# Two transformer blocks on one core: who sums the squares of a norm, who writes its diagonal, and where the rms of the first feed-forward goes

## What is computed

```python
def rmsnorm(x, g):
    y = x * lax.rsqrt(jnp.mean(x * x, axis=-1, keepdims=True) + EPS)
    return y * g

def first_block(x, ...):                       # 512 tokens
    for layer in range(2):
        h = rmsnorm(x, pre_norm[layer])
        if layer == 0:
            y = (retention(rope(q), rope(k), v) * silu(gate)) @ w_out_a   # q, k, v, gate from h @ w_in_a
        else:
            kv = rmsnorm(x, kv_norm) @ w_kv    # k (with rope) and v
            y = (rmsnorm(diff_attention(q, k, v, lam), sub_norm) * silu(gate)) @ w_out_b
        x = x + rmsnorm(y, post_norm[layer])
    return x

def swiglu(x, w_gate, w_up, w_down):
    return (silu(x @ w_gate) * (x @ w_up)) @ w_down

def second_block(x, ...):
    h = concatenate([meta, x])                 # 528 tokens
    h = h + 0.5 * swiglu(rmsnorm(h, ffn1_norm), ...)
    u = rmsnorm(h, mix_norm)                   # then mla(u) and gated_deltanet(u), merged by gates
    h = h + merged @ w_out
    h = h + 0.5 * swiglu(rmsnorm(h, ffn2_norm), ...)
    return rmsnorm(h, final_norm)[:, 16:]
```

## Time and profile before

| | before |
|---|---|
| median of three runs, us | 2071.51 (2068.78 to 2074.17) |
| profiled execution, us | 2070.14 |
| its span in the profile, us | 2068.1 |
| TensorE busy, us | 2013.0 (97%) |
| weight loads busy, us | 1760.6 (85%) |
| VectorE busy, us | 1093.9 (53%) |
| ScalarE busy, us | 838.6 (41%) |
| GpSimd busy, us | 599.9 (29%) |
| mean granted TensorE clock | 0.996 |

### The profile page before, as it was taken

One profiled execution on the slowest core, in us unless ns is written; L12 is line 12 of the kernel. 1 busy time (PEld: TensorE's weight loads), 2 busy tenths in 40 slices (PEclk: granted clock), 3 DMA queues, 4 the chain that ended last, 5 costly groups with the idle time before them and its releaser, 6 DMA issues. The chain is left out here.

```text
span 2068.1 us, 33871 instructions
## 1 busy us (share of the span) xinstructions
PE 2013.0 (97%) x14432; PEld 1760.6 (85%) x14432; DVE 1093.9 (53%) x1618; ACT 838.6 (41%) x1330; POOL 599.9 (29%) x207
## 2 busy tenths in 40 slices
PE   8999999999999999999999999999999999999998
PEld 6899888778977688999999878898777787999897
DVE  4400576236256737774656242266566556847473
ACT  6332222336456634452435344343222333444353
POOL 4443332444320134211202322034235243020202
PEclk9999999999999999999999999999999999999999
DMA  5323121222311121323232431132113121423331
GB/s 177 100 84 111 58 77 61 93 80 82 102 62 42 42 62 42 110 89 108 83 123 82 104 90 44 32 99 62 43 58 119 62 82 61 138 87 113 100 99 57
DMA packets 170062, 171.64 MB, mean 83 GB/s; under 512 B 16940, under 2 KB 160680, under 8 KB 169912
## 3 DMA queue, kind: packets, MB, share of 16 engines
q1 hardware_dynamic: 168508, 167.25, 25.8%
q10 hardware_dynamic: 1404, 2.23, 0.3%
HBM read 163.17 MB, written 6.29 MB: 82 GB/s over the span
## 5 line engine op out<-in xcount | busy, mean ns | idle before, releaser
L784 POOL TENSOR_TENSOR w_lo<-w_raw,w_hi 128x2048 fp32r<-128x2048 f32 (+2 forms) x117 | 493.7, 4223 | 1018.7 <-ACT w_hi L927 592.2
L2367 PE MATMUL ps<-u_hi,w_hi 128*128 128x512 f32 (+2 forms) x1480 | 477.1, 343 | 11.5 <-DVE sg L1867 3.3
L2367 PE MATMUL ps<-u_hi,w_lo 128*128 128x512 f32 (+2 forms) x1472 | 470.3, 339 | 0.0
L2367 PE MATMUL ps<-u_lo,w_hi 128*128 128x512 f32 (+2 forms) x1472 | 462.9, 339 | 1.0 <-DVE u_lo L1520 0.8
L2367 PEld LDWEIGHTS ps<-u_hi,w_hi 128*128 128x128 f32 x1480 | 267.7, 189 | 41.8 <-issue 5.5
L2367 PEld LDWEIGHTS ps<-u_lo,w_hi 128*128 128x128 f32 x1472 | 265.1, 189 | 31.2 <-DVE u_lo L1520 5.5
L2367 PEld LDWEIGHTS ps<-u_hi,w_lo 128*128 128x128 f32 x1472 | 266.6, 189 | 27.7 <-issue 0.5
L927 ACT ACTIVATE w_hi<-w_raw 128x2048 fp32r<-128x2048 f32 (+2 forms) x157 | 247.8, 1580 | 64.1 <-PE ps L2367 58.1
L2367 PE MATMUL ps<-hidden_hi,w_hi 128*128 128x264 f32 (+1 forms) x528 | 140.9, 321 | 1.3 <-DVE hidden_lo L1850 1.3
L2367 PE MATMUL ps<-hidden_lo,w_hi 128*128 128x264 f32 (+1 forms) x528 | 140.9, 321 | 0.0
L2367 PE MATMUL ps<-hidden_hi,w_lo 128*128 128x264 f32 (+1 forms) x528 | 140.6, 320 | 0.0
(11 more groups left out here) (423 smaller groups left out, 4010.6 us busy)
## 6 DMA issues: line engine op xcount, KB each, us to landing
w_raw<-in_w_in_a SPq DMA_DIRECT2D x22, 1024.0 KB, 5.2
w_raw<-in_ffn_w_gate SPq DMA_DIRECT2D x22, 1024.0 KB, 5.3
w_raw<-in_ffn_w_up SPq DMA_DIRECT2D x22, 1024.0 KB, 5.3
w_raw<-in_ffn_w_down SPq DMA_DIRECT2D x24, 768.0 KB, 4.5
w_raw<-in_w_in SPq DMA_DIRECT2D x17, 1024.0 KB, 5.3
w_raw<-in_w_out_a SPq DMA_DIRECT2D x8, 1024.0 KB, 5.1
w_raw<-in_w_kv SPq DMA_DIRECT2D x8, 1024.0 KB, 5.4
w_raw<-in_w_in_b SPq DMA_DIRECT2D x8, 1024.0 KB, 5.4
```

The lines of the kernel that those rows point to most:

```text
L784: pool.tensor_tensor(WL[:, u % RAWS, part], RAW[:, u % RAWS, part], WH[:, u % SPLITS, part].bitcast(F32), ALU.subtract).then_inc(lo_done, 1)
L2367: return nc.tensor.matmul(o, a, b, start=start, stop=stop, **kw)
```

## The change

- In post0 and post1, VectorE adds only the first seven squares. TensorE sums that (`two_sums`), runs 2 fillers in place of 5, and sums the eighth square straight from `SQ`, into the same columns.
- In ffn1, VectorE adds no squares. TensorE sums each of the eight squares as it comes (`square_sums`), inside the first unit, between the hi and the lo products of each contraction step. The final sums and the 9 fillers go. `spread_after` becomes 4: no slot is set aside, and the spread goes to columns 264 to 439 of three banks (three pieces of 176), behind step k = 3 of the second unit's chunk m = 0. The copy of the rms reads it there, and the bank of that slot is released with the first of the normalising instructions.
- The diagonal of post0, norm1, post1, ffn1, mix and ffn2 goes from ScalarE to VectorE (`diagonal_on_vector`), as products of the broadcast identity with the broadcast root, in two pieces (three in ffn1); the spread waits for each piece on its own. norm0, cq and ckv stay with ScalarE.
- ScalarE's order in ffn1: each square follows its `u_hi`, and the conversion of the first coming weight follows the eight squares.

```diff
-            ffns[name] = [(job(part, spread_after=3 if name == "ffn1" and n == 0 else None), job(4, kc=part))
+            ffns[name] = [(job(part, spread_after=4 if name == "ffn1" and n == 0 else None), job(4, kc=part))
...
+        not_added = {norms[name][3] + KC - 1 for name in ("post0", "post1", "ffn1")}
+        def added_upto(q):
+            return len([x for x in range(q + 1) if x not in not_added])
+        PIECES = {"ffn1": 3}
+        def pieces_of(name):
+            return 1 if name in ("norm0", "cq", "ckv") else PIECES.get(name, 2)
+        def diags_before(name):
+            return sum(pieces_of(x) for x in list(norms)[:norms[name][0]] if x != "final")
...
+            if name == "ffn1":
+                return PS[:, 2:5, 264:440]
...
-            diagonal("post0")
             for k in range(KC):
                 act.wait_ge(res_done, k + 1)
                 u_hi("norm1", k)
             for k in range(KC):
                 squares_after("norm1", k)
-            diagonal("norm1")
...
-                    next_hi(jg, 0, j)
+                    if (name, j) != ("ffn1", 0):
+                        next_hi(jg, 0, j)
...
-            diagonal("post1")
             for k in range(KC):
                 act.wait_ge(res_done, KC + k + 1)
                 u_hi("ffn1", k)
-            for k in range(KC):
                 squares_after("ffn1", k)
-            diagonal("ffn1")
+            hi(ffns["ffn1"][0][0].unit0 + 2)
             ffn_act("ffn1", 0, "mix")
-            diagonal("mix")
...
+            def diagonal_on_vector(name):
+
+                n, cols = norms[name][:2]
+                k, w = token_tiles(width_of(cols))
+                g = k // pieces_of(name)
+                dve.wait_ge(root_done, n + 1)
+                dve.wait_ge(nb_done, n)
+                for a in range(pieces_of(name)):
+                    nc.vector.tensor_tensor(DIAG[0:w, a * g * w:(a + 1) * g * w].rearrange("p (t c) -> p t c", t=g),
+                                            IDENT[0:w, 0:w].unsqueeze(1).to_broadcast([w, g, w]),
+                                            STAT[0:w, 2, a * g:(a + 1) * g].unsqueeze(2).to_broadcast([w, g, w]),
+                                            ALU.mult).then_inc(diag_done, 1)
...
+                    nc.vector.tensor_copy(RSTDB[:, 0:width].rearrange("p (a n) -> p a n", a=3),
+                                          spread_over(name)).then_inc(rb_done, 1)
...
                 rstd(name)
+                diagonal_on_vector(name)
...
+                    if after != "ffn1":
+                        add_square(q0 + k, k == 0, width_of(cols))
                 rstd(after)
+                diagonal_on_vector(after)
...
-            for k in range(KC):
+            for k in range(KC - 1):
...
+                    if k == 0 and name == "ffn1":
+                        slot, _ = spread_chunk(ffns[name][0][0])
+                        last.then_inc(ps_free[slot], 1)
...
             rstd("mix")
+            diagonal_on_vector("mix")
...
             rstd("ffn2")
+            diagonal_on_vector("ffn2")
...
+                                if after == "ffn1" and not high:
+                                    square_sums(after, k)
...
-                            if jb.spread_after is not None and k == kc - 2:
-                                slot_free(pe, *spread_chunk(jb))
-                                norm_sums(after)
-                            if jb.spread_after is not None and k == kc - 1:
-                                keep_clock(2 * spread_chunk(jb)[0], 9)
                             if k == kc - 1 and after == "norm1":
                                 norm_sums(after)
-                            elif k == kc - 1:
+                            elif k == (SPREAD_K if after == "ffn1" else kc - 1):
                                 norm_spread(after)
...
+            def square_sums(name, k):
+
+                _, cols, _, before, _ = norms[name]
+                count, w = token_tiles(width_of(cols))
+                pe.wait_ge(sq_done, before + k + 1)
+                for t in range(count):
+                    last = mm(sums_at[0:w, t:t + 1], SQ[:, (before + k) % 2, t * w:(t + 1) * w], ONES[:, 0:1],
+                              start=(k, t) == (0, 0), stop=k == KC - 1, skip_group_check=True)
+                last.then_inc(ns_done if k == KC - 1 else sq_added, 1)
+
+            def two_sums(name, between):
+
+                n, cols, squares, before, _ = norms[name]
+                k, w = token_tiles(width_of(cols))
+                pe.wait_ge(sq_added, added_upto(before + KC - 2))
+                for t in range(k):
+                    mm(sums_at[0:w, t:t + 1], SUMSQ[:, t * w:(t + 1) * w], ONES[:, 0:1], start=t == 0, stop=False,
+                       skip_group_check=True)
+                between()
+                pe.wait_ge(sq_done, before + KC)
+                for t in range(k):
+                    last = mm(sums_at[0:w, t:t + 1], SQ[:, (before + KC - 1) % 2, t * w:(t + 1) * w], ONES[:, 0:1],
+                              start=False, stop=True, skip_group_check=True)
+                last.then_inc(ns_done, 1)
...
-                pe.wait_ge(diag_done, n + 1)
-                o = spread_over(name)
-                if k == NT:
-                    last = mm(o, ONES[0:w, :], DIAG[0:w, 0:SEQ])
-                else:
-                    for a in range(2):
-                        last = mm(o[:, a, :], ONES[0:w, :], DIAG[0:w, HALF * a:HALF * (a + 1)])
+                o, made = spread_over(name), pieces_of(name)
+                parts = 2 if k > NT and made == 1 else made
+                size = k * w // parts
+                for a in range(parts):
+                    pe.wait_ge(diag_done, diags_before(name) + min(a + 1, made))
+                    last = mm(o[:, a, :] if k > NT else o[:, a * size:(a + 1) * size], ONES[0:w, :],
+                              DIAG[0:w, a * size:(a + 1) * size])
                 last.then_inc(nb_done, 1)
...
-            keep_clock(idle_bank, 5)
-            norm_sums("post0")
+            two_sums("post0", lambda: keep_clock(idle_bank, 2))
             keep_clock(idle_bank, 10)
```

More of the change, by code:

```diff
@@ L77, in build @@
         FIRST, LAST = 16512, 229344
+        SPREAD_K = 3
         ends, starts = {None: FIRST}, {}
@@ L407, in build @@
                    "mix": 6 * KC, "ffn2": 7 * KC, "final": 8 * KC, "cq": QN_ROW, "ckv": KVN_ROW}
+        not_added = {norms[name][3] + KC - 1 for name in ("post0", "post1", "ffn1")}
[6 more added lines that the diff above has]
+            return sum(pieces_of(x) for x in list(norms)[:norms[name][0]] if x != "final")
         def gain(name, k):
             return GAINS[:, gain_of[name] + k:gain_of[name] + k + 1]
-        slot, _ = spread_chunk(ffns["ffn1"][0][0])
+        first_slots = [(ffns["ffn1"][0][0].chunk0 + n) % SLOTS for n in range(4)]
         cq_bank = 2 * (j_cq.chunk0 % SLOTS) + 1
-        assert slot == 0 and cq_bank == 5
+        assert first_slots == [1, 2, 3, 0] and spread_chunk(ffns["ffn1"][0][0])[0] == 1 and cq_bank == 5
         spread_banks = {"post0": [2 * ((j_kv_k.chunk0 + 2) % SLOTS) + 1],
                         "post1": [2 * ((ffns["ffn1"][0][0].chunk0 + 2) % SLOTS) + 1],
-                        "ffn1": [2 * slot, 2 * slot + 1], "mix": [cq_bank, cq_bank + 2], "cq": [cq_bank - 2],
+                        "mix": [cq_bank, cq_bank + 2], "cq": [cq_bank - 2],
                         "ckv": [cq_bank - 4, cq_bank - 2]}
         def spread_over(name):
+            if name == "ffn1":
+                return PS[:, 2:5, 264:440]
             banks = spread_banks.get(name, [1])
@@ L969, in square @@
                 if q >= 2:
-                    act.wait_ge(sq_added, q - 1)
+                    act.wait_ge(sq_added, added_upto(q - 2))
                 nc.scalar.activation(halves(SQ[:, q % 2, 0:width]), src, ACT.Square).then_inc(sq_done, 1)
@@ L1465, in _ @@
                     squares_after("ffn2", 2 * j + m)
-            diagonal("ffn2")
             ffn_act("ffn2", 1, "final")
@@ L1482, in add_square @@
                 else:
-                    dve.wait_ge(sq_added, q)
+                    dve.wait_ge(sq_added, added_upto(q - 1))
                     nc.vector.tensor_tensor(SUMSQ[:, 0:width], SUMSQ[:, 0:width], SQ[:, par, 0:width],
@@ L2519, in norm_sums @@
                 else:
-                    pe.wait_ge(sq_added, before + squares)
+                    pe.wait_ge(sq_added, added_upto(before + squares - 1))
                 for t in range(k):
@@ L2681, in _ @@
             idle_bank = next(b for b in (3, 5, 7) if b not in spread_banks["post1"])
-            keep_clock(idle_bank, 5)
-            norm_sums("post1")
+            two_sums("post1", lambda: keep_clock(idle_bank, 2))
             keep_clock(idle_bank, 10)
```

5 lines of the change are left out of this document (removed).

## The result

The changed kernel took 2075.32 us (median of 19 executions, 2070.68 to 2078.18) against 2071.51: a ratio of 1.0015, interval 1.0008 to 1.0022, so slower by a little, and clear of noise. The profiled execution took 2072.63 us, its span is 2070.7. (One correction to what stands ahead of the prediction: a call of `keep_clock` is two passes in the trace, not four, and the four matmuls of a sum are eight; the prediction counted them right.)

A forecast was written before the change was run, and what follows sets the result against it. TensorE was taken as the bound, busy nearly the whole span. Posts -1.4, norm1 +1.2, ffn1 -0.4, mix 0 and ffn2 +0.75 give +0.15 us on the 2071.51 median: 2071.7 predicted, range 2067.0 to 2076.0.

The forecast's parts named there:

- the collision: At norm1, ffn1, mix, ffn2: GpSimd's 4.60 us split starts behind the root and holds VectorE's diagonal until it ends.
- Rival (a): The port does not hold the diagonals, as VectorE's requests get in first: -3.5 us, 2068.0; chance 0.17.
- The posts: post0 and post1: earlier sums, fewer fillers and VectorE's diagonal start the spread 0.7 us earlier each, bounds 0.2 and 1.1.
- norm1: Held diagonal, then second split on the diff_rope scaling: third kv_k unit +1.85 us, 0.6 given back later, +1.2 in all.
- ffn1: Final sums and fillers go, square sums enter the first unit, held diagonal idles TensorE: -0.4 us, or -3.5 if nothing held.
- the price of the twelve passes: ffn1's first unit: square sums add 0.89 us to each contraction step of 1.47, making 2.36; bounds 0.89 and 1.03.
- The wait at the spread: ffn1: the first diagonal piece comes only at the split's end, 808.15, so TensorE idles 3.1 us.
- ffn2 and mix: ffn2's held diagonal makes TensorE 0.75 us later; mix's comes in time even if held a whole split: 0.
- the half clock behind before's wait: ffn1: 0.50 of full clock in 811 to 814 counted as removed; 1.45 us to add if it halves again.
- rival (b): norm1's second split slips between the diagonal pieces, 2.4 us worse (2074.1); with half clock in ffn1 2075.5; chance 0.16.
- (c): Single-column passes in ffn1's first unit let the clock fall there, some 10 us more: 2082; chance 0.05.
- (d): Squares cheaper or spare columns free more; posts at 1.1, nothing held, norm1 0, ffn1 -4: -6.5, 2065.0; chance 0.04.

The follow-up runs named there:

- GpSimd behind VectorE: Changed kernel with GpSimd's splits waiting for VectorE's diagonal (norm1, ffn1, ffn2) and for the rotation table's scalings: 2063.10 us (0.9968), again 2062.31 us (0.9961).
- norm1's diagonal alone: Kernel before, with only norm1's diagonal moved from ScalarE to VectorE: 2073.03 us, 1.0008 of before.
- the later spread: Changed kernel with ffn1's spread behind step k = 7 instead of k = 3 of the second unit: 2074.64 us, 1.0012 of before.
- one operand: Changed kernel with VectorE's diagonals made block by block, identity times a scalar for each partition: 2077.76 us, 1.0031 of before.
- ffn1's filler alone: Changed kernel with 11 more keep_clock calls ahead of ffn1's spread only: 1.0005 of before.
- the diagonal first: Changed kernel with GpSimd's splits waiting for the diagonal in norm1, ffn1 and ffn2, but not for the rotation table's scalings: 2068.53 us, 0.9986 of before.
- norm1's filler alone: Changed kernel with 8 more keep_clock calls ahead of the third unit of the keys only: 1.0007 of before.
- posts: Kernel before, with only post0 and post1 changed (last square summed by TensorE, 2 fillers for 5, VectorE's diagonal): 2067.64 us, 0.9983 of before.
- ScalarE's diagonals: Changed kernel with the diagonals of norm1, ffn1, mix and ffn2 back on ScalarE ahead of its weight conversion: 2067.33 us, 0.9989 of before.
- both fillers: Changed kernel with 8 more keep_clock calls ahead of the keys' third unit and 11 ahead of ffn1's spread: 2070.81 us, 0.9993 of before.

## Why the prediction was right, and where it was 3 us short

**What bounds it, and the collision.** Right in every row that it named: GpSimd's split begins behind the root, VectorE comes 0.06 us later and waits to the split's end, in norm1, ffn1 and ffn2 (5.19, 5.18 and 5.17 us). Rival (a) falls with these rows, and the runs with GpSimd behind VectorE show the cause: GpSimd waits for the pieces, and they take 0.8 us. The Trainium skill ("SBUF — State Buffer", section "SBUF: two separate sides") has the loser wait for the whole instruction; the trace agrees (a first piece of 4.85 us under a split of 4.63).

**The posts.** -0.7 each was forecast, -1.01 measured, within the stated bounds. The mis-sized term is the sum: it was taken at 0.92, the distance between the issues at 775.78 and 776.70, where TensorE had just waited. Running on from a product the eight passes take 0.81 (773.07 to 773.88), twice. That moves the ten fillers up by 0.2, and the diagonal (0.76 for both pieces) is no later than they: the spread stands 4.46 behind the end of the products (773.07 to 777.53) in place of 5.38 (774.21 to 779.59), 0.92 less. The last 0.1 comes behind it, where the spread in two halves and the 12 fillers issue in 3.46 in place of 3.56.

**norm1.** +1.2 forecast, +1.27 measured, by the steps named: third unit +1.87 (forecast +1.85), 0.60 given back at the fourth (0.6). Less the 0.98 by which this run is ahead, the pieces were forecast done at 478.27 and the scaling at 483.87; they were at 478.32 and 483.86. The second split did fall on the scaling, 3.82 us for the two products.

**ffn1.** -0.4 forecast, +0.05 measured. The step that was too small is the price of the twelve passes in a contraction step: 2.43 from one set to the next (782.05 to 784.48) where 2.36 was forecast, eight times 0.07. The passes themselves take 0.89 to the next issue as before; the rest is in the products around them. The wait at the spread was forecast at 3.1 and is 2.87.

**ffn2 and mix.** +0.75 against +0.82, 0 against 0.

**The sum and the clock.** The sum of the norms came out at +0.12, where +0.15 was forecast. That it is so close is luck: the posts were off by -0.62, ffn1 by +0.45, norm1 and ffn2 by +0.07 each. What failed is the step in ffn1 that counted the half clock behind before's wait as removed with this wait, and gave the chance of it falling again only to rival (b). The prediction itself had put a wait of 3.1 us into ffn1, and its third unit, 1.85 us late behind an unchanged filler, meant another at norm1. The fourteen traces, one execution each, show what follows such waits. Ahead of norm1's third unit TensorE waits 1.7 us or more in seven of them, and half clock comes with it in four; in the seven where it waits 1.02 or less there is none. In ffn1 it waits 2.4 us or more in eight, before among them, and half clock follows in seven; in the six with 0.98 or less there is none. Filler in both takes back about 5 us, more than the whole difference from before. By the trace with half clock in both places a full price is +2.79 - 1.27 = 1.5 us at norm1 and 1.61 - 0.05 = 1.6 at ffn1. Before paid ffn1's as well, so the new loss by these rows is at most some 1.5 us in an execution, and the mean loss that the clock shows is 2.0.

**What stays open.** The filler took back more than these two places explain, and norm1's diagonal alone, with a wait of 1.70 us, lost no mean clock. In the profiles, half clock at 1638, and a stretch twice as long at 1348, stand only in kernels that keep a wait at norm1 or ffn1 (the changed one twice, the later spread, one operand, ffn1's filler alone; the longer stretch also with the diagonal first and with norm1's filler alone), and in none of the others (before, posts, norm1's diagonal, ScalarE's diagonals, both fillers, GpSimd behind VectorE twice). But norm1's diagonal alone, before and the posts have such a wait too, and speak against it. These stages are not touched by the change and do the same work in all; whether it is the moment at which they come that decides, or chance in one profile for each kernel, can't be told from these runs.

**The rivals.** (b)'s mechanism, the second split between two pieces, did not happen in the changed kernel but did with one operand, at +5.8 for the third unit. (c) did not come: the clock stood at 1.00 through the square sums of every trace. (d) did not come, since the splits held the pieces; its own terms add up to -6.2, not to the -6.5 that it states.

## What to carry to other kernels

When work is moved from an engine that waited to another one, ask what the first will now do earlier, and whom that releases: here ScalarE's freed conversion made GpSimd's long split ready at the very moment at which VectorE's short product was due. A short operation on the path that shares a resource with a long one off the path wants an order by semaphore: GpSimd's waits at four places, 0.9 us long behind the roots and 2.0 ahead of the second split of the keys, were together worth about 11 us, of which the last one made 4 to 5. And a wait of TensorE is not priced at its length alone: two to three idle microseconds in a full stream were here followed by half clock in some executions and not in others, at 1.5 to 1.6 us each time, so that a forecast which adds a wait has to add that too, with its chance.

## What was not expected of the hardware

A product of VectorE with one tensor operand and a scalar for each partition, 0.27 us by itself, is held by GpSimd's split just as one with two operands (first block 4.64 us). The Trainium skill ("SBUF — State Buffer", section "SBUF: two separate sides") counts instructions in a mode that uses both ports among those held; no run here shows which mode this product was in.

That the same two waits lost no clock in one profile and 1.5 to 1.6 us each in the next was the other surprise: nine of the changed kernel's 30 executions lie above 2076 us and four below 2072, with nothing changed but the granted clock.
